# A third projection unit chain inside the adaptive norm's loads, and the x transposes moved ahead of it

## What is computed

```python
mod = jnp.einsum('bd,de->be', jax.nn.silu(c), w_ada) + b_ada
shift, scale, gate = jnp.split(mod, 3, axis=-1)
h = rmsnorm(x, ln_gain) * (1 + scale[:, None]) + shift[:, None]
proj = jnp.einsum('btd,de->bte', h, w_in)
q_a, ckv, krope, g_a, q_b, k_b, v_b, q_i, k_i, w_i, g_b = jnp.split(proj, split_at, axis=-1)
```

## Time and profile before

| | us |
|---|---|
| median of 3 runs | 1039.85 |
| the three runs | 1036.28 to 1043.31 |
| profiled execution | 1037.61 |
| its span | 1035.7 |
| TensorE busy | 954.8 (92%) |
| VectorE busy | 419.0 (40%) |
| ScalarE busy | 338.3 (33%) |
| GpSimd busy | 91.3 (9%) |

### The profile page before, as it was taken

One profiled execution on the slowest core, in us unless ns is written; L12 is line 12 of the kernel. 1 busy time (PEld: TensorE's weight loads), 2 busy tenths in 40 slices (PEclk: granted clock), 3 DMA queues, 4 the chain that ended last, 5 costly groups with the idle time before them and its releaser, 6 DMA issues.

```text
span 1035.7 us, 14400 instructions
## 1 busy us (share of the span) xinstructions
PE 954.8 (92%) x5851; PEld 821.7 (79%) x5851; DVE 419.0 (40%) x857; ACT 338.3 (33%) x621; POOL 91.3 (9%) x165
## 2 busy tenths in 40 slices
PE   3799689999999999999999999999998999699995
PEld 0466377899998788888998998899887897588884
DVE  2223243336431244432325712368334353863453
ACT  2332242333312243223314522333322244542332
POOL 1000013102100000111111100010011001300000
PEclk9999799999999999999999999999999999899998
DMA  8999946565533234564336665345657428764323
GB/s 320 385 313 354 329 162 184 144 156 152 154 112 92 68 94 134 153 190 138 115 100 217 208 203 167 104 133 184 224 166 236 157 83 298 207 203 136 122 62 122
DMA packets 128402, 183.28 MB, mean 177 GB/s; under 512 B 29408, under 2 KB 79256, under 8 KB 127184
## 3 DMA queue, kind: packets, MB, share of 16 engines
q1 hardware_dynamic: 115744, 138.71, 43.1%
q0 software_dynamic: 12592, 43.65, 12.6%
HBM read 171.80 MB, written 10.52 MB: 176 GB/s over the span
## 4 chain that ended last, share of the span: by engine, by line
PE 82%; DMA 5%; DVE 4%; ACT 4%; issue 2%; SPq 2%; POOL 1%; ACTq 0%; POOLq 0%; DVEq 0%
PE proj L1606 32%; PE proj L1617 31%; DMA raw<-in_w_in 2%; SPq L637 2%; PE bankO L1597 1%; PE bankO L1695 1%; PE bankO L1704 1%; PE bankO L1920 1%; PE proj L1597 1%; DMA raw<-in_w_ada 1%; PE bankS L1821 1%; DVE w_lo L1187 1%; ACT w_hi L859 1%; PE bankT L1836 1%; PE bankO L1798 1%
## 5 line engine op out<-in xcount | busy, mean ns | idle before, releaser
L1187 DVE TENSOR_TENSOR w_lo<-raw,w_hi 128x1024 fp32r<-128x1024 f32 (+2 forms) x168 | 198.6, 1186 | 241.0 <-ACT w_hi L859 240.3
L859 ACT ACTIVATE w_hi<-raw 128x1024 fp32r<-128x1024 f32 (+2 forms) x168 | 171.8, 1027 | 220.8 <-PE proj L1606 130.9
L1606 PE MATMUL proj<-w_hi,hT_hi 128*128 128x512 f32 (+2 forms) x528 | 207.6, 393 | 24.7 <-DVE w_lo L1187 12.7
L1617 PE MATMUL proj<-hT_hi,w_hi 128*128 128x384 f32 x640 | 222.1, 347 | 1.1 <-ACT misc L859 1.1
L1617 PE MATMUL proj<-hT_hi,w_lo 128*128 128x384 f32 x640 | 214.5, 335 | 0.0
L1617 PE MATMUL proj<-hT_lo,w_hi 128*128 128x384 f32 x640 | 214.4, 335 | 0.0
L1606 PE MATMUL proj<-w_hi,hT_lo 128*128 128x512 f32 (+2 forms) x528 | 202.9, 384 | 0.0
L1606 PE MATMUL proj<-w_lo,hT_hi 128*128 128x512 f32 (+2 forms) x528 | 202.6, 384 | 0.0
L1606 PEld LDWEIGHTS proj<-w_hi,hT_hi 128*128 128x128 f32 x528 | 102.0, 193 | 46.8 <-DVE w_lo L1187 15.7
L1617 PEld LDWEIGHTS proj<-hT_hi,w_hi 128*128 128x128 f32 x640 | 120.6, 188 | 9.1 <-issue 7.0
L1617 PEld LDWEIGHTS proj<-hT_lo,w_hi 128*128 128x128 f32 x640 | 120.6, 188 | 0.7 <-issue 0.2
(11 more groups left out here) (308 smaller groups left out, 936.3 us busy)
## 6 DMA issues: line engine op xcount, KB each, us to landing
raw<-in_w_in SPq DMA_DIRECT2D x104, 512.0 KB, 3.8
raw<-in_w_ada SPq DMA_DIRECT2D x128, 256.0 KB, 6.6
raw<-in_w_ada SPq DMA_DIRECT2D x32, 512.0 KB, 3.8
raw<-in_w_out SPq DMA_DIRECT2D x32, 512.0 KB, 3.8
raw<-in_w_in SPq DMA_DIRECT2D x32, 256.0 KB, 3.2
raw<-in_w_in SPq DMA_DIRECT2D x32, 128.0 KB, 2.5
wuk<-in_w_uk POOLq DMA_DIRECT2D x16, 256.0 KB, 3.7
kload<-in_cache_dsa_k POOLq DMA_DIRECT2D x8, 512.0 KB, 5.0
```

What stands on the lines that cost most here:

```text
L859: return nc.scalar.activation(out, in_, func, scale=scale, **kw)
L1187: V.tensor_tensor(w_lo[:, u % RAW, 0:w], raw[:, u % RAW, 0:w], w_hi[:, n % SPLIT, 0:w].bitcast(F32), ALU.subtract).then_inc(lo_ready, 1)
L1606: ins = mm(banks[t][:, 0:ncol], a[:, kt, rows], w[:, n, :], start=first and n == m == 0, stop=final and n == per - 1 and m == 2)
L1617: ins = mm(banks[blk][:, 0:TOK], w[:, n, cols], a[:, kt, :], start=first and n == m == 0, stop=final and n == per - 1 and m == 2)
```

## The change

The chunk `ga` 1 moves from the dense units to the front. The new order of units in a quarter from the second on: five of `ada`, one of `kb`, five of `ada`, one of `ga` 0, six of `ada`, and behind the quarter's last unit one of `kb` and one of `ga` 1, while the quarter's `modT` and `h` steps run. So 5 units of `kb`, 3 of `ga` 0 and 2 of `ga` 1 lie before the last `ada` unit (unit 73, before it was unit 70), and six behind it.

`ga` 1 accumulates in banks S and T. For this all twelve `xT` are put in the first quarter, one behind each unit from unit 6 on and the last three around its end; `modT` goes to bank O, which it shares with the sums of `ada`, so that a quarter's first unit waits until `modT` of the quarter before has been read. `uvT` 0 and `ckT` 0 wait until `ga` 1 has been copied out, and the `w_uv` loads and `uvT` start three units later. In the dense part four units fewer stand, so five `gate` units instead of three are left at the end.

```diff
--- before.py
+++ after.py
@@ -63,10 +63,10 @@
 def chunks():
 
     out = [("ada", q, 1, 1) for q in range(4)]
-    out += [("kb", 0, 2, NT), ("ga", 0, 4, 2), ("ckv", 0, 2, NT), ("m0", 0, 2, NT), ("m1", 0, 2, NT)]
+    out += [("kb", 0, 2, NT), ("ga", 0, 4, 2), ("ga", 1, 4, 2), ("ckv", 0, 2, NT), ("m0", 0, 2, NT), ("m1", 0, 2, NT)]
     out += [("qn", j, 4, 2) for j in range(4)]
     out += [("kb", 1, 2, NT)] + [("vb", j, 2, NT) for j in range(2)]
-    out += [("ga", j, 4, 2) for j in range(1, 4)]
+    out += [("ga", j, 4, 2) for j in range(2, 4)]
     for kind in ("qi", "qb", "gb"):
         out += [(kind, j, 4, 2) for j in range(4)]
     out += [("gate", r, 1, 1) for r in range(2)]
@@ -87,20 +87,17 @@
         c = CHUNK_OF[kind, j]
         return [(c, k) for k in range(KT // CHUNKS[c][2])]
 
-    keys, gates = of("kb", 0), of("ga", 0)
+    keys, first, second = of("kb", 0), of("ga", 0), of("ga", 1)
     out = of("ada", 0)
     for q in range(1, 4):
         ada = of("ada", q)
-        out += ada[:6] + [keys[2 * q - 2]]
-        if q < 3:
-            out += ada[6:10] + [gates[q - 1]] + ada[10:13] + [keys[2 * q - 1]] + ada[13:]
-        else:
-            out += ada[6:]
-    out += [keys[5], gates[2], keys[6], keys[7], gates[3]]
-    ga1, gate0 = CHUNK_OF["ga", 1], CHUNK_OF["gate", 0]
-    for c in range(CHUNK_OF["ckv", 0], ga1):
+        out += ada[:5] + [keys[2 * q - 2]] + ada[5:10] + [first[q - 1]] + ada[10:]
+        out += [keys[2 * q - 1], second[q - 1]]
+    out += [keys[6], keys[7], first[3], second[3]]
+    ga2, gate0 = CHUNK_OF["ga", 2], CHUNK_OF["gate", 0]
+    for c in range(CHUNK_OF["ckv", 0], ga2):
         out += of(*CHUNKS[c][:2])
-    dense = [u for c in range(ga1, gate0) for u in of(*CHUNKS[c][:2])]
+    dense = [u for c in range(ga2, gate0) for u in of(*CHUNKS[c][:2])]
     gate = of("gate", 0) + of("gate", 1)
     for n, u in enumerate(dense):
         out.append(u)
@@ -130,6 +127,8 @@
             mine = [4]
         elif (kind, j) == ("ga", 0):
             mine = [3, 4]
+        elif (kind, j) == ("ga", 1):
+            mine = [NPB + 1, NPB + 2]
         elif nb == 2:
 
             mine = [0, 1] if out[-1][0] == 2 else [2, 3]
@@ -147,7 +146,7 @@
 
 
 STEP_BANKS = {
-    "gains": "S", "bias": "O", "xT": "T", "uvT": "S", "modT": "S", "ckT": "T", "kiT": "S", "qrT": "T", "qrsT": "TO",
+    "gains": "S", "bias": "O", "xT": "T", "uvT": "S", "modT": "O", "ckT": "T", "kiT": "S", "qrT": "T", "qrsT": "TO",
     "ukT": "T", "kn": "O", "vm": "O", "mp": "S", "mt": "T", "mv": "O", "ql": "O", "krc": "T",
     "st": "T", "ss": "S", "sp": "S", "so": "O", "oa": "O", "ysq": "O",
     "kic": "T", "ip": "S", "is": "T", "iacc": "O", "kl": "TO", "dp": "S", "dt": "T", "dv": "O",
@@ -174,28 +173,28 @@
 
     put(0, ("ld_x", 0))
     put(1, ("ld_small", 0))
-    run(5, "xsq", NT)
-    put(8, ("xr", 0))
-    run(9, "xT", NT)
+    run(3, "xsq", NT)
+    put(5, ("xr", 0))
+    run(6, "xT", 9)
     put(12, ("gains", 0))
-    for g in range(1, 4):
-        for t in range(NT):
-            put(LAST_UNIT["ada", g - 1] + (3, 5, 11)[t], ("xT", NT * g + t))
+    u = LAST_UNIT["ada", 0]
+    put(u, ("xT", 9), ("modT", 0), ("xT", 10))
+    put(u + 1, ("xT", 11))
 
     for q in range(4):
         u = LAST_UNIT["ada", q] + 1
-        put(u, ("modT", q))
+        if q:
+            put(u, ("modT", q))
         for n in range(MQ):
-            v = u + (1, 1, 2, 2)[n] if q < 3 else u + n // 2
-            put(v, ("h", MQ * q + n))
-            put(v + 1, ("hl", MQ * q + n))
+            put(u + n // 2, ("h", MQ * q + n))
+            put(u + n // 2 + 1, ("hl", MQ * q + n))
     u = LAST_UNIT["ada", 3]
     put(u + 4, ("ld_const", 0))
     put(u + 4, ("bias", 0))
     put(u + 8, ("bias_rd", 0))
     for n in range(HEADS):
-        put(u + 2 + 2 * n, ("ld_uv", n))
-        put(u + 5 + 2 * n, ("uvT", n))
+        put(u + 5 + 2 * n, ("ld_uv", n))
+        put(u + 8 + 2 * n, ("uvT", n))
 
     u = LAST_UNIT["ckv", 0] + 1
     put(u, ("ckn", 0))
@@ -512,7 +511,7 @@
 
     ps = [nc.alloc_psum_tensor(f"proj{n}", [P, 512], F32) for n in range(NPB)]
     bank = {n: nc.alloc_psum_tensor(f"bank{n}", [P, 512], F32) for n in "STO"}
-    ps.append(bank["O"])
+    ps += [bank["O"], bank["S"], bank["T"]]
 
 
     bias_d = nc.dram_tensor("bias_scratch", [HEADS, NDELTA], F32).ap()
@@ -529,7 +528,7 @@
 
     raw_loaded = [sem(f"raw_loaded{n}") for n in range(RAW)]
     hi_ready, lo_ready, unit_used = sem("hi_ready"), sem("lo_ready"), sem("unit_used")
-    proj_free = [sem(f"proj_free{n}") for n in range(NPB + 1)]
+    proj_free = [sem(f"proj_free{n}") for n in range(NPB + 3)]
     full = {b: sem(f"bank_{b}_full") for b in "STO"}
     free = {b: sem(f"bank_{b}_free") for b in "STO"}
 
@@ -1216,9 +1215,9 @@
             emptied(dve, "gains", 0)
             b_cols = gcol[:, 32:64].rearrange("p (a k) -> p a k", a=2)[:, :, MQ * n:MQ * (n + 1)]
             for a in range(2):
-                ins = V.tensor_tensor(part[:, a], bank["S"][:, P * a:P * (a + 1)].rearrange("p (k j) -> p k j", j=32)[:, :, 0:9],
+                ins = V.tensor_tensor(part[:, a], bank["O"][:, P * a:P * (a + 1)].rearrange("p (k j) -> p k j", j=32)[:, :, 0:9],
                                       b_cols[:, a].unsqueeze(2).broadcast_to([P, MQ, 9]), ALU.add)
-            ins.then_inc(free["S"], 1)
+            ins.then_inc(free["O"], 1)
             emptied(dve, "modT", n)
             V.scalar_tensor_tensor(out=part[:, 1], in0=part[:, 1], scalar=1.0, in1=gcol[:, MQ * n:MQ * (n + 1)]
                                    .unsqueeze(2).broadcast_to([P, MQ, 9]), op0=ALU.add,
@@ -1582,7 +1581,12 @@
                 if first and BEFORE[c][n]:
                     pe.wait_ge(proj_free[BANKS[c][n]], BEFORE[c][n])
 
-            if (kind, j) in (("kb", 0), ("ga", 0)) or kind == "wo":
+            if kind == "ada" and first and j:
+                emptied(pe, "modT", j - 1)
+            if (kind, j) == ("ga", 1) and first:
+                emptied(pe, "gains", 0)
+                emptied(pe, "xT", 11)
+            if (kind, j) in (("kb", 0), ("ga", 0), ("ga", 1)) or kind == "wo":
 
                 pe.wait_ge(sem("hT_ready"), per * (k + 1) + (KT if kind == "wo" else 0))
             if kind in WHOLE:
@@ -1638,6 +1642,8 @@
 
         def uvT(h_):
             pe.wait_ge(sem(f"wuv_in{h_ % 2}"), 16 * (h_ // 2 + 1))
+            if h_ == 0:
+                moved(pe, "ga", 1)
             out = take("uvT", h_, "S")
             for q in range(CB):
                 ins = tr(out[:, P * q:P * (q + 1)], wuv[:, h_ % 2, P * q:P * (q + 1)], eye[:])
@@ -1645,13 +1651,15 @@
 
         def modT_(n):
             moved(pe, "ada", n)
-            out = take("modT", n, "S")
+            out = take("modT", n, "O")
             for a in range(2):
                 ins = tr(out[:, P * a:P * (a + 1)], modA[:, n % 2, P * a:P * (a + 1)], eye[:])
-            ins.then_inc(full["S"], 1)
+            ins.then_inc(full["O"], 1)
 
         def ckT(t):
             pe.wait_ge(sem("ckvn_ready"), NT)
+            if t == 0:
+                moved(pe, "ga", 1)
             out = take("ckT", t, "T")
             for q in range(CB):
                 ins = tr(out[:, P * q:P * (q + 1)], ckvn[:, t, P * q:P * (q + 1)], eye[:])
```

## The result

| | before | changed |
|---|---|---|
| median, us (20 runs each, side by side) | 1040.27 | 1044.43 |
| range, us | 1034.51 to 1043.88 | 1037.57 to 1050.73 |
| ratio, 95% interval | | 1.0049 (1.0029 to 1.0069) |
| span of the profiled execution, us | 1035.7 | 1044.2 |

The changed kernel is slower by half a per cent: 4.2 us by the medians, 5.1 us (3.0 to 7.2) by the ratio. The sum had been +4.3, the forecast 1043. A second series against before gave 1.0048 (1.0027 to 1.0068).

The account below looks back on a forecast made before the run. TensorE is busy nearly all the time, but the early `w_ada` stage is bound by loads through 8 slots. 15.7 − 12.6 − 1.2 + 2.4 = +4.3 us on 1037.6 gave 1041.9; adjusted towards the median, 1043 was predicted, range 1030 to 1054.

Parts of the forecast that it names:

- The sum: Whole kernel: later last `w_ada` product, less projection work and idle time behind it, plus the tail: +4.3 us.
- The first quarter: Start: transposes 2.00 us apart delay the first `kb` unit from 49.21 to 58.6 us, and loads pause until 64.6.
- The last `w_ada` product: End of the `w_ada` loading stage: last product at 138.1 us instead of 122.4, 15.7 us later.
- two projection units in a row at each quarter's end: Third and fourth quarters: the pair's second unit holds its slot, pausing loads, so each quarter takes 31.1 us.
- The refill: After a pair releases its slot: the next load lands 4.6 us later, bounds 3.8 to 5.4.
- rival B: Pairs at quarters' ends: half clock after idle gaps adds +5 to +9 us, so 1048 to 1052; chance 0.16.
- What was gained: Behind the last `ada` unit: three fewer projection units, −12.6 us, and a shorter wait before the next projection, −1.2 us.
- The waits for `hT_lo`: After the last `modT`: two waits totalling 3.0 us stay, with the same steps in the same order.
- The tail: Around `w_out`: +3.5 us waiting for bank 4, −1.1 us for two `gate` units moved into idle time, sum +2.4.
- Rival A: First stage: loads don't pause and the kernel is faster, 1029 to 1031 us, if first `kb` starts before 51; chance 0.13.
- Rival C: Stores through `stage`: a chain of three blocks ScalarE, `uvT` 0 and splits wait, +4 to +6 us, 1048; chance 0.11.

Follow-up runs that it names:

- run 1: The kernel before with only all twelve x transposes moved into the first quarter: ratio to before 1.0084, 8.7 us.
- run 2: The changed kernel with the transposes alternating between banks T and S: ratio to before 1.0026, 2.4 us below the changed kernel.
- run 6: The changed kernel with the second quarter's first `kb` unit behind nine `ada` units, not five, first `ga` behind thirteen, not ten: ratio to before 0.9993.
- run 4: The changed kernel with all four `ga` 1 units behind the last `w_ada` unit, one `kb` unit alone at each quarter's end: ratio to before 1.0240.
- run 7: The changed kernel with the second and third quarters' end pairs broken, the `kb` unit three `ada` units ahead of the end: ratio to before 1.0132.
- run 3: The changed kernel with two more `gate` units among those of `qi` 2 and 3, leaving three at the end: ratio to before 1.0015.
- run 9: The kernel of run 8 with the fourth quarter's `ga` 0 unit moved behind the last `w_ada` unit: ratio to before 1.0010.
- run 5: The changed kernel itself timed again, unedited, against the kernel before: ratio 1.0048, profiled span 1041.0 us.
- run 8: The changed kernel with transposes in two banks, first `kb` unit behind nine `ada` units, three `gate` units at the end: 1031.13 us, ratio to before 0.9921.

## Why the prediction was right, and where it wasn't

**The first quarter: right.** Cycle of the transposes 2.00 forecast, 1.91 measured; first `kb` matmul 58.6, measured 56.43; idle time ahead of it 5.5, measured 5.90; its end 64.6, measured 62.1; a pause of the loads at about 60, measured 42 GB/s from 60 to 64. Most of the 2.2 us by which it came early are the start of the transposes (25.30, forecast 26.3) and the clock, which rose within the second one (1.27 us instead of 2.08). Runs 1, 2 and 6 show each link: transposes alone +8.7 us, a shorter cycle −2.4 (3.3 us earlier in the profile, the time not clear of the noise), loads let past the waiting unit −5.1.

**The last `w_ada` product: mechanism half wrong, size too small.** The sum had 138.1 us, measured 142.87. The step "two projection units in a row at each quarter's end" gave every quarter 31.1 us, set by loads that wait for the pair's second unit. The second quarter ended at 73.14 (forecast 75.9); from last product to last product the third took 38.0 us and the fourth 31.7. Three things in the step were off.

- *What ends a quarter.* In the third and the fourth quarter it was not the last loads but the `ga` unit in the middle: its load landed at 99.01 and 131.74, then came its split, 2.4 us, the unit itself, 7.05 and 6.00 us, and six `ada` units without a gap, 2.8 us. That is 12.2 and 11.1 us from the landing to the last product, where the sum had six more loads and a product, 8.8.
- *The refill.* The sum had 4.6 us, with bounds of 3.8 and 5.4. From the end of the pair's second unit (86.64, 120.29) to the landing of the `ga` load, with four loads at 1.357 us taken off, it was by my estimate 6.9 and 6.0. The page of before has a median of 6.6 us for the `w_ada` loads, which the prediction passed over.
- *What a pair covers.* The `h` steps stand ahead of the next split in ScalarE's program. The step priced what the pair holds, and not what it covers. Runs 4 and 7 show the sign: with the pair's second unit taken away the kernel is 20 and 9 us slower.

In the third quarter the units at 76.23 and 101.40 also ran in part at the low clock (5.99 and 7.05 us), in the fourth the one at 134.14 (6.00); the sum had a slow unit only at the start, and rival B those of the pairs.

**What was gained: −12.6 right in kind, the second term too small.** I gave 1.2 us for the shorter wait ahead of `kb` unit 5. In the changed kernel the wait was 0.47 us: six `ada` units were done without a gap up to 142.87 and the `kb` unit stood nearly ready behind them. So 4.53 − 0.47 = 4.1 us of idle time went, and with them the low clock of the unit behind it, 6.99 − 4.42 = 2.6 us: −6.6 in place of −1.2. This makes up for the 4.8 us by which the stage's end was off: 20.5 − 12.6 − 6.6 = +1.3, against +1.9 in the sum and 1.15 between the marks. The two errors cancel since they are one fact: at the end of the stage TensorE, and not the loads, was behind.

**The waits for `hT_lo`:** 3.0 forecast, 3.6 measured, at one place instead of two. **The tail:** +3.5 us of wait forecast, +3.7 measured; run 3 gives 3.5 us for all of it, 3 us either way. TensorE idles there for 7.2 + 4.5 us instead of 3.8 + 5.1; the larger part now stands ahead of the first `wo` unit, for its `w_lo`.

**The total: right, and in part by luck.** The sum was +4.3, the medians give +4.2 and the ratio +5.1 us. But the sum put the middle at nothing, and there the nine profiles of kernels with `ga` 1 in front lose 3.3 us on average; at the start it had 0.8 us more than the first profile of the change shows and 2.5 us more than the second. The stated range, 1030 to 1054, was to end where rival B does, but B's own paragraph ends at 1052.

**Rival A** (no pause) fell with the first `kb` matmul at 56 us, its limit was 51. **Rival B** (low clock at each pair) held at one pair of three: the pair at 76.23 began slow, those at 111.09 and 143.34, with 0 and 0.47 us of idle time before them, ran at the full clock (4.38 and 4.42 us). The low clock fell on other units too: the `ga` unit at 101.40 took 7.05 us instead of 4.20 behind 3.14 us of idle time, the units at 76.23 and 134.14 took 6.0 behind 3.09 and 2.60, and the first `kb` unit 5.71 behind 5.90. Against 4.38 and 4.20 us at full clock, the low clock cost 1.3 + 1.6 + 2.9 + 1.8 = 7.6 us in this stage, in place of 1.6 + 1.6 + 2.6 = 5.9 before (the prediction had passed over one of these, the unit at 107.50): 1.7 us more than before already paid. The rule of the Trainium skill ("TensorE: Matmul & The Clock Gate", HAM oscillation — how this bites in real kernels), by which a matmul burst shorter than the wait for its load can fall back to the low clock at every tile, is seen only in part: four of the twelve projection units from 56.43 to 152 us ran in part at the low clock. **Rival C** (stores): `ga` 1 was copied at 182.90, 15.9 us after `kb` 0 (166.99), forecast 15 to 16; TensorE waited 0.7 us there, for `wuv`. It cost nothing in the changed kernel, 1.2 us in run 4 and 3.6 us in run 9.

Of what the sum lacks in the middle only a wait of 1.5 us for `wuk` has a name. It stands in this profile and, with 0.3 to 1.5 us, in those of runs 2, 4, 5, 6, 8 and 9, but not in those of runs 3 and 7. I had not followed GpSimd's queue behind `uvT`, which now comes later; that this is the cause is not shown.

## What to carry to other kernels

A waiting instruction costs time through the buffers that stand full behind it, too. Ahead of a unit that can't start yet, put the short units whose loads free a slot (here −5.1 us for one edit of the order), and put long ones where another engine has a serial chain to finish (here 9 us for the pairs of units over the `h` steps). Work done only to make room for a change, like the transposes here (+8.7 us), is to be priced first: it was at least as large as the whole loss of the change. A second bank, a later first unit and two `gate` units moved away from the end made the same change 0.8% faster than the kernel before.

## What the runs showed of the hardware

- Gaps of nearly the same length ahead of a unit ended differently in the granted clock: in the changed kernel 3.14 us led to a unit of 7.05 us and 2.60 us to one of 6.00; before the change 2.71 us led to one at full speed (79.24) and 2.72 us to one of 6.01 us (107.50). In run 6 even 1.84 us led to a unit of 6.00 (72.35), and 2.28 us in the changed kernel to one at full clock (124.87, 4.38 us). A price per gap is an average.
- At line 1928 of the changed kernel, and at the same place in the others, TensorE waits 1.8 to 2.2 us in six of twelve profiles (the changed kernel's and those of runs 1, 3, 4, 6 and 7), put down to no releaser; in the others the wait is 1.1 to 1.4 us and put down to `pnew`. In the two profiles of the changed program this and the load of `wuk` made up 0.7 and 1.2 us of a difference of 3.2 us. A single profile can carry such amounts in a stretch that a change never touched, and the series of runs can't be replaced by it.
